# The norms' factor 1/sqrt(variance): square root and reciprocal, or logarithm and exponential

## The reference

```python
def rms_norm(x, g):                      # first block: before its FFN, and at its end
    y = xf * lax.rsqrt(jnp.mean(xf * xf, axis=-1, keepdims=True) + NORM_EPS)
    return y * g
def layer_norm(x, g, b):                 # second block, three times in each of two layers
    mu = mean(xf); var = mean(square(xf - mu))
    return (xf - mu) * lax.rsqrt(var + LN_EPS) * g + b
x = rms_norm(x + g1 * (y @ w_out), ...)                          # norm 1
x = rms_norm(x + g2 * swiglu(modulate(...)), final_g)            # norm 2
for l in range(2):
    x = layer_norm(ALPHA * x + 0.5 * swiglu_2(x, ...), ...)      # norms 3 and 6
    mix = hybrid_mixer_2(x, ...)
    x = layer_norm(ALPHA * x + mix, ...)                         # norms 4 and 7
    x = layer_norm(ALPHA * x + 0.5 * swiglu_2(x, ...), ...)      # norms 5 and 8
```

## Time and profile before

| | |
|---|---|
| median of three runs | 3265.61 us (3264.32 to 3267.36) |
| profiled execution | 3267.23 us, its span 3265.4 us |
| TensorE (PE) busy | 3207.4 us, 98% |
| VectorE (DVE) busy | 1756.7 us, 54% |
| ScalarE (ACT) busy | 1473.8 us, 45% |
| GpSimd (POOL) busy | 1730.8 us, 53% |
| granted TensorE clock, mean | 0.997 of full speed |

### The profile page before, as it was taken

One profiled execution on the slowest core, in us unless ns is written; L12 is line 12 of the kernel. 1 busy time (PEld: TensorE's weight loads), 2 busy tenths in 40 slices (PEclk: granted clock), 3 DMA queues, 4 the chain that ended last, 5 costly groups with the idle time before them and its releaser, 6 DMA issues.

```text
span 3265.4 us, 56909 instructions
## 1 busy us (share of the span) xinstructions
PE 3207.4 (98%) x19910; PEld 2858.1 (88%) x19910; DVE 1756.7 (54%) x2931; ACT 1473.8 (45%) x2585; POOL 1730.8 (53%) x1330
## 2 busy tenths in 40 slices
PE   7999999999999999999999999999999999999998
PEld 5778898999899989888888998899888888889987
DVE  5864885773267715344137771577244352177724
ACT  5544555454255523256235552455232473245533
POOL 2343114666466646545446664576555454466654
PEclk9999999999999999999999999999999999999999
DMA  7342002223222322323222333222323332222332
GB/s 293 132 157 70 1 2 81 100 103 116 85 85 103 122 97 86 96 90 107 98 87 79 107 110 103 72 103 103 116 78 104 97 98 96 97 78 97 108 111 84
DMA packets 90053, 322.38 MB, mean 99 GB/s; under 512 B 9776, under 2 KB 12208, under 8 KB 89776
## 3 DMA queue, kind: packets, MB, share of 16 engines
q1 hardware_dynamic: 88576, 316.65, 28.6%
q10 hardware_dynamic: 1328, 3.67, 0.3%
HBM read 318.19 MB, written 2.10 MB: 98 GB/s over the span
## 4 chain that ended last, share of the span: by engine, by line
PE 88%; DVE 6%; ACT 2%; issue 2%; POOL 2%; DMA 0%; SPq 0%; POOLq 0%; DVEq 0%; ACTq 0%
PE ps L665 10%; PE ps L666 10%; PE ps L670 10%; PE ps L1301 9%; PE ps L1309 9%; PE ps L1303 9%; PE ps L1234 3%; PE ps L1341 3%; PE ps L1339 3%; PE ps L1346 3%; PE ps L1369 2%; PE ps L1365 2%; PE ps L1363 2%; PE ps L1147 2%; DVE ps L2641 1%
## 5 line engine op out<-in xcount | busy, mean ns | idle before, releaser
L530 POOL TENSOR_TENSOR w_lo<-raw,w_hi 128x512 fp32r<-128x512 f32 x726 | 997.2, 1397 | 1060.7 <-ACT w_hi L1512 1060.0
L1512 ACT ACTIVATE w_hi<-raw 128x1024 fp32r<-128x1024 f32 x363 | 384.0, 1060 | 947.9 <-PE ps L670 486.6
L666 PE MATMUL ps<-acts,w_hi 128*128 128x512 f32 x1336 | 519.8, 389 | 0.0
L665 PE MATMUL ps<-acts,w_hi 128*128 128x512 f32 x1336 | 519.8, 389 | 0.0
L589 POOL TENSOR_TENSOR w_lo<-raw,w_hi 128x512 fp32r<-128x512 f32 x270 | 376.0, 1406 | 153.1 <-ACT w_hi L1901 153.1
L1301 PE MATMUL ps<-acts,w_hi 128*128 128x256 f32 x1440 | 364.0, 285 | 9.2 <-DVE tmp L2696 5.6
L1303 PE MATMUL ps<-acts,w_hi 128*128 128x256 f32 x1440 | 360.9, 283 | 0.0
L670 PE MATMUL ps<-acts,w_lo 128*128 128x512 f32 x1336 | 329.9, 389 | 0.0
L670 PEld LDWEIGHTS ps<-acts,w_lo 128*128 128x128 f32 x1336 | 250.8, 188 | 52.1
L666 PEld LDWEIGHTS ps<-acts,w_hi 128*128 128x128 f32 x1336 | 250.8, 188 | 51.9
L665 PEld LDWEIGHTS ps<-acts,w_hi 128*128 128x128 f32 x1336 | 250.8, 188 | 51.8
(11 more groups left out here) (453 smaller groups left out, 7137.7 us busy)
## 6 DMA issues: line engine op xcount, KB each, us to landing
raw<-stream SPq DMA_DIRECT2D x543, 512.0 KB, 3.4
ada_behind<-ada SPq DMA_DIRECT2D x32, 512.0 KB, 3.5
ada_first<-ada SPq DMA_DIRECT2D x8, 1024.0 KB, 14.1
X<-x_in ACTq DMA_DIRECT2D x1, 2048.0 KB, 8.4
out<-X SPq DMA_DIRECT2D x16, 128.0 KB, 1.7
xin<-x_in ACTq DMA_DIRECT2D x2, 768.0 KB, 6.8
xin<-x_in SPq DMA_DIRECT2D x2, 768.0 KB, 9.1
rope_sb<-rope SPq DMA_DIRECT2D x1, 1280.0 KB, 9.0
```

What stands on the lines that cost most here:

```text
L530: last = nc.gpsimd.tensor_tensor(w_lo[:, slot, part, :], raw[:, slot % RAW, part, :], f32(w_hi[:, slot, part, :]), ALU.subtract)
L665: mm(o, w_hi[:, s, k, :], xh, start=start, stop=False, skip_group_check=True)
L666: mm(o, w_hi[:, s, k, :], xl, start=False, stop=False, skip_group_check=True)
L1512: A(w_hi[:, s, :, :], raw[:, s % RAW, :, :], ACT.Copy).then_inc(s_hi, 1)
```

## The change

In `root`, ScalarE takes the logarithm in place and then the exponential of -0.5 times it, which is written straight to the place where VectorE's reciprocal went. `link` adds a wait of ScalarE for its own instruction before. The reciprocal is gone. The instruction that loads a table ahead of time is a logarithm. The mean's square goes to `tmp[1]` in place of `tmp[0]`, and the first two `centre` instructions of a half read the negative mean from `tmp[0]` in SBUF in place of PSUM.

```diff
-LAYER_STEPS = 156
+LAYER_STEPS = 150
@@ ScalarE, norm @@
-                A(epsc[:, 7:8], epsc[:, 0:1], ACT.Sqrt)
+                A(epsc[:, 7:8], epsc[:, 0:1], ACT.Ln)
@@ ScalarE, root @@
                     if mean:
                         act.wait_ge(s_var, var.up())
-                        A(spread, spread, ACT.Sqrt, bias=epsc[:, 4:5]).then_inc(s_std, 1)
+                        link(A(spread, spread, ACT.Ln, bias=epsc[:, 4:5]))
                     else:
                         act.wait_ge(s_stat, stat.up())
-                        A(spread, spread, ACT.Sqrt, scale=1.0 / D, bias=epsc[:, 0:1]).then_inc(s_std, 1)
+                        act.wait_ge(s_pre, pre.now)
+                        link(A(spread, spread, ACT.Ln, scale=1.0 / D, bias=epsc[:, 0:1]))
+                    A(ps[n.moments[h]][:, HALF:LAT], spread, ACT.Exp, scale=-0.5).then_inc(s_std, 1)
@@ VectorE, half @@
-                    def centre(k):
-                        TT(X[:, k, tokens], X[:, k, tokens], negative, ALU.add).then_inc(s_dve, 1)
+                    def centre(k, moved=negative):
+                        TT(X[:, k, tokens], X[:, k, tokens], moved, ALU.add).then_inc(s_dve, 1)
                         centred[k] = step.up()
...
-                        link(TT(tmp[0][:, tokens], negative, tmp[0][:, tokens], ALU.mult))
-                        STT(stats[:, HALF:LAT], stats[:, HALF:LAT], 1.0 / D, tmp[0][:, tokens], ALU.mult,
+                        link(TT(tmp[1][:, tokens], negative, tmp[0][:, tokens], ALU.mult))
+                        STT(stats[:, HALF:LAT], stats[:, HALF:LAT], 1.0 / D, tmp[1][:, tokens], ALU.mult,
                             ALU.subtract).then_inc(s_var, 1)
-                        centre(0)
-                        centre(1)
+                        centre(0, tmp[0][:, tokens])
+                        centre(1, tmp[0][:, tokens])
                     between(-1)
                     dve.wait_ge(s_std, std.up())
-                    link(V.reciprocal(factor, stats[:, HALF:LAT]))
```

## The result

The changed kernel takes 3272.34 us (median of nine runs, 3270.99 to 3275.66), the kernel before 3264.63 us (nine runs, the three already known among them, 3262.67 to 3267.36): ratio 1.0023, 95% interval 1.0015 to 1.0032. It is 7.7 us slower. The forecast was 3274.0 with a range of 3268 to 3278, and "slower by over 0.2%" had 0.70. Its main case happened.

A forecast was written before the change was run, and what follows sets the result against it. TensorE, busy 98% of the span, was taken as the bound, with delays reaching it through GpSimd's low tiles. Terms 4.0 + 2.1 + 1.0 + 0.1 + 0.9 + 0.3 = 8.4 us on 3265.61 gave 3274.0, range 3268 to 3278.

The forecast's parts named there:

- A load before each exponential and each second logarithm: ScalarE in root: 24 table loads, 16 before exponentials and 8 before second halves' logarithms, 30.8 us of ScalarE's time.
- The copy 1.70 us later, norms 3, 5, 6 at 1.33 each: First halves: w_hi copy 1.70 us later, 0.37 taken by GpSimd's slack, 1.33 reaching TensorE; three norms, 4.0 us.
- Norms 4 and 7, 1.04 each: GpSimd's low_part 1.70 us later, less slack of 0.59 and 0.07: 1.04 each, 2.1 us together.
- Norms 1 and 2: The copy 1.19 and 1.44 us later, partly taken by GpSimd's slack or idle time: costs of 1.0 and 0.1 us.
- Second halves covered: Second halves of norms: the loads make rows 1.2 us later in norm 3, but this does not reach TensorE.
- Rival C: Second halves' 1.2 us comes through in norms 1, 2, 3, 5 and 6: 6 us more, 3280; chance 0.05.
- the two covers: Norm 3's second half: GpSimd's own lateness covers the delay by 0.3 us, TensorE's remaining first-half work by 3 us.
- Norm 8, 0.9: Last norm, nothing behind it: second half's two loads put VectorE's first row at 3257.97 instead of 3257.07, +0.9 us.
- `centre` from SBUF, 0.3: Second halves of norms 3, 5 and 6: GpSimd reads SBUF beside the pair; 0.1 us each, 0.3 in all.
- Rival A: No load between logarithm and exponential in root: -2.2 us in all, 3263.4; chance 0.08.
- Rival B: TensorE or GpSimd takes up half of the first copy's delay through unseen slack: 4.5 us, 3270.1; chance 0.17.

The follow-up runs named there:

- one_set: The changed kernel, but the load ahead of each norm names the one table set that holds both functions: 3263.83 us, ratio 0.9998 to the kernel before.
- delay_copy: The kernel before, with an exponential on one column put between root(0) and the copy to w_hi: 3270.52 us, ratio 1.0020.
- copy_first: The changed kernel, all loads kept, with the first copy w_hi ahead of root(0) in norms 2, 3, 5, 6 and 8: 3268.19 us, ratio 1.0008.
- second_only: The changed kernel with logarithm and exponential in the second halves alone, square root and reciprocal in the first: 3266.20 us, ratio 1.0006.
- before_centre: The kernel before with only the mean's square in the second scratch tile and each half's first two centre instructions reading from SBUF: 3268.19 us, ratio 1.0010.
- mean_copy_first: one_set_ordered with the first copy w_hi ahead of root(0) in norms 3 to 8: 3257.18 us, ratio 0.9977 to the kernel before.
- one_set_ordered: The changed kernel with one table set, centre reading from PSUM and the exponential waiting for the second centre instruction: 3264.75 us, ratio 0.9994 to the kernel before.
- ordered: The changed kernel, loads kept, with centre reading from PSUM again and the exponential waiting for the second centre instruction: 3274.96 us, ratio 1.0028 to the kernel before.

## Why the prediction was right

Its mechanism held at the steps that make the sum; what follows is where its sizes stood. Two things made the number look better or worse than they were. The sum was 8.4 us and the norms lost 7.6: norm 8 was set 0.56 too high, norms 3, 5 and 6 together 0.35 too high, norms 4 and 7 together 0.32 too low, so a part cancelled. And 1.0 of the 1.7 us between 3274.0 and 3272.34 is the base: the median of before was 3265.61 over three runs and 3264.63 over nine.

- **A load before each exponential and each second logarithm.** Right: 24 loads at 1.283 us. The Trainium skill (ScalarE: Activation LUTs, section "Table sets: the hidden batching unit") speaks of one set for both functions. Such a set exists, as one_set shows: preloaded by name, it leaves `root` without a load. The changed kernel does not get it by itself: each of its two functions is loaded anew when the other has run. ScalarE's busy time grew by 35.9 us, where some 37 were said.
- **The copy 1.70 us later, norms 3, 5, 6 at 1.33 each.** Measured: 1.66 later, and +1.34, +1.25, +1.35. The 0.03 is the exponential, taken as 0.40 and measured as 0.37. Norm 3's 1.34 holds about 0.1 for `centre`, as predicted. delay_copy and copy_first show that it is this path. TensorE's wait was split as described, with 0.81 for line 530 in the first feature tile.
- **Norms 4 and 7, 1.04 each.** Measured +1.24 and +1.16. GpSimd in norm 4 of the changed kernel:

```profile
1714.40 2.72 POOL L530 TENSOR_TENSOR w_lo<-raw,w_hi 128x512 fp32r<-128x512 f32 x2 [9.30 <-ACT w_hi L1512]
1717.08 1.60 POOL L614 TENSOR_TENSOR acts<-X,acts 128x256 fp32r<-128x256 f32 x2
1718.64 2.73 POOL L530 TENSOR_TENSOR w_lo<-raw,w_hi 128x512 fp32r<-128x512 f32 x2
```

  Both low_parts take longer, 2.72 and 2.73 against 2.54 and 2.60: in each, the second of the two instructions now runs beside VectorE's sum of the squares (line 2537, two SBUF inputs). The step held durations fixed that depend on the neighbour. That this is the reason follows from the timeline; no run isolates it.
- **Norms 1 and 2.** 1.0 and 0.1 against +0.90 and +0.04.
- **Second halves covered.** Right as to TensorE: second_only loses 0.3 in norms 3, 5 and 6, which is the slow `centre` pair (before_centre has the same 0.3) and no load. Rival C is out. But of the two covers only TensorE's held throughout. In norm 5 of the changed kernel the first row waits for the pair, not for the factor, which was there at 2085.87; GpSimd then sits idle for 1.97 us ahead of the second half's low tiles, and TensorE still does not wait. VectorE:

```profile
2083.62 4.27 DVE L2573 TENSOR_TENSOR X<-X,tmp 128x256 f32<-128x256 f32 x2
2087.81 0.47 DVE L2594 SCALAR_TENSOR_TENSOR ps<-X,prm,ps 128x256 f32<-128x256 f32 x1
```

- **Norm 8, 0.9.** Too much; +0.34. ScalarE in its second half:

```profile
3257.68 1.05 ACT L1512 ACTIVATE w_hi<-raw 128x1024 fp32r<-128x1024 f32 x1
3258.75 1.28 ACT L1824 ACT_TABLE_LOAD   x1
3260.04 0.45 ACT L1824 ACTIVATE ps<-ps,epsc 128x256 f32<-128x256 f32 x1
3260.51 1.28 ACT L1829 ACT_TABLE_LOAD   x1
3261.80 0.37 ACT L1829 ACTIVATE ps<-ps 128x256 f32<-128x256 f32 x1
```

  From the first load to the row it is 3.45 us, with 3.53 forecast, but the first row came 5.02 after the variance's first step (3257.18) where it was 4.18 before (3252.89 to 3257.07): +0.84. The first half gave 0.17 of it back, so the row came 0.67 later counted from the first root. The tail from VectorE's last rows to the end is 0.34 us shorter than in the profile of before (3.65 against 3.99). This is no chance of one execution: it is 3.6 us in every kernel here that has logarithm and exponential in at least one half, and 3.9 to 4.2 in the four that have square root and reciprocal in both. Behind ScalarE's last row only the store of the result is left; why it ends sooner stays open.
- **`centre` from SBUF, 0.3.** The size was right by luck and the reason wrong. It was argued that VectorE loses nothing, since the pair takes 0.74 us and ends long before the factor, and that GpSimd loses little, since its low_part took 2.52 to 2.60 whatever stood beside it. But VectorE slows, from 0.74 to 1.61, 2.85 and 4.27 us in the second halves of the changed kernel. In norms 3 and 8 the loads hide it, in norm 5 TensorE's remaining work. GpSimd slows too where the pair took 1.61: in norm 3 its four low tiles took 3.00 us in place of 2.83 and the low_part behind them 2.73 in place of 2.56. In norm 5, with the pair at 4.27, it did not slow, and that norm lost 0.1 less. Without the loads the pair costs more: 3.0 us in before_centre, which keeps the reciprocal, and 1.39 net in norm 8 of one_set. The slow pair is also why VectorE's busy time fell by 18.5 us and not by 28: at 17.2 us for 24 instructions it took some 7 more than at 0.41 each. The row for GpSimd said nothing of VectorE.
- **Rival A** (3263.4) is what one_set is, but for the `centre` pair: 3263.83. **Rival B** is out, since nothing of the delay was taken up beyond the slack that was counted.

## What to carry to other kernels

Ask of each instruction that is made longer what stands behind it on its engine, and not only who uses its result: here, in norms 3, 5 and 6, the result came 0.17 us earlier, and the kernel lost 7.7 us, nearly all of it by a copy of weights queued behind it. Functions that alternate on ScalarE are to be counted with a load each, unless the trace shows none, and one set for both is worth asking for by name. And put work that needs only weights ahead of an instruction that will wait.

## What was not expected of the hardware

**Two SBUF inputs beside GpSimd.** The same two instructions, X<-X,tmp on 128x256, took 0.75 us with GpSimd idle, 1.61 in the second half of norm 3, 2.85 in norm 8, 4.27 in norm 5, and 4.26 in norm 3 of one_set, where GpSimd worked until 1260.25:

```profile
1256.62 4.26 DVE L2573 TENSOR_TENSOR X<-X,tmp 128x256 f32<-128x256 f32 x2
```

Of these 4.26 us the first instruction took 3.93 and the second 0.41. With one input from PSUM they stayed at 0.74 beside the same work. GpSimd lost far less: in norm 8 its low_part went from 2.49 to 2.66.

The Trainium skill (SBUF — State Buffer, section "SBUF: two separate sides") says that a VectorE instruction with two SBUF inputs and a GpSimd instruction that reads SBUF compete for one pair of ports, and that whichever starts first holds it for the whole instruction. The trace agrees in size in norm 8: the two instructions of 2.85 us, 2.10 more than alone, stood beside low_parts of 1.25 us each. The 3.93 us of the one instruction are more than any single GpSimd instruction beside it (1.29 at most): four of them ended while it stood. How the turn is given is not shown. This rule spoke against the `centre` part of the change and would have priced it at the length of GpSimd's instructions.

**TensorE's clock in norms 4 and 7.** Stretches of the kernel before; the number before the last two is the granted clock:

```profile
1720.00:1724.00 4.00, 2.64 (x11) 2.46 (x12) 3.20 (x8) 4.00 (x11) 4.00 (x5) 0.72 0.41 133
1724.00:1728.00 4.00, 4.00 (x25) 3.65 (x25) 1.93 (x5) 0.60 (x3) 3.42 (x5) 0.85 0.32 114
2900.00:2904.00 4.00, 3.56 (x28) 3.31 (x27) 3.46 (x7) 0.80 (x2) 3.36 (x5) 1.00 0.34 118
```

After its waits (0.18, 0.69 and 1.41 us) TensorE ran a part of norm 4 at the lower of its two levels, and norm 7, with the same three waits and one of 0.44 more, did not. That is the likely cause of the 0.76 us between 28.51 and 27.75 in the table. It came and went between executions: in one_set norm 7 had it (28.49). In mean_copy_first, with waits of 1.40 and 0.43 us alone, both norms had 1.00. When it strikes is open.

**A wait that comes in numbers.** TensorE's waits for `tmp` in the down projections, of one_set and then of one_set_ordered (same line, shifted by one):

```profile
PE ps L1301 <- DVE tmp L2697: 4.6, 9, 0.5
```

```profile
PE ps L1302 <- DVE tmp L2702: 6.8, 13, 0.5
```

Each is 0.5 us, and the kernels had between 9 and 13 of them with no change near. The four more make 2.2 us. One_set_ordered's profiled span (3262.8) is 1.7 us longer than one_set's (3261.1), though its norms are 1.2 us shorter in sum; these waits are most of the 2.9 us between. For changes of a few us, single norms in the trace say more than the total.

**Loads and waits.** The load of a second half started as soon as ScalarE was free, before the logarithm's own wait was over (at 1257.48 in norm 3 of the changed kernel, the logarithm at 1259.05 released by VectorE). The load in `ordered`, whose exponential has an added wait, started only after that wait. Why the two differ was not tried.
